# The last add level of the even transform residues in the product tables, and the skip weight in the first filter tap

## The reference

```
filt = hdn @ w4                                   # (length, 2 orders, 2 directions, 1024)
filt = filt * exp(-t * deltas)                    # t runs from 0 to 1, so the factor is 1 at tap 0
kcirc = concat([h_fwd, 0, h_bwd[:0:-1]])          # 2 * length taps
spec = rfft(z, 2 * length) * rfft(kcirc)
y = irfft(spec)[:length] + z * skip               # skip: one weight for each channel and order
zz = hx1 * long_conv(hv, filt[0], skip[0]);  zz = hx2 * long_conv(zz, filt[1], skip[1])
```

## Time and profile before

| | us |
|---|---|
| median of 3 runs | 3003.19 |
| the profiled execution | 3002.44 |
| its span | 3000.4 |
| PE busy | 2732.0 (91%) |
| DVE busy | 1526.7 (51%) |
| POOL busy | 411.0 (14%) |

### The profile page before, as it was taken

One profiled execution on the slowest core, in us unless ns is written; L12 is line 12 of the kernel. 1 busy time (PEld: TensorE's weight loads), 2 busy tenths in 40 slices (PEclk: granted clock), 3 DMA queues, 4 the chain that ended last, 5 costly groups with the idle time before them and its releaser, 6 DMA issues.

```text
span 3000.4 us, 33511 instructions
## 1 busy us (share of the span) xinstructions
PE 2732.0 (91%) x13372; PEld 1569.4 (52%) x13372; DVE 1526.7 (51%) x2153; ACT 813.9 (27%) x1672; POOL 411.0 (14%) x501
## 2 busy tenths in 40 slices
PE   5999999999999999788888888789399999999997
PEld 3444444766776666545555544445144444444487
DVE  6444331333323232389999999787482222222243
ACT  5333222343434334312222221112151111100132
POOL 0000000000000000133333334333010000000000
PEclk8999999999999999789999999899699999999999
DMA  5522221010101010300111111210631131000022
GB/s 208 204 81 94 82 81 50 26 50 26 51 27 49 26 50 16 117 25 32 32 60 60 32 35 42 84 50 28 207 109 49 43 116 39 15 28 29 29 91 85
DMA packets 103770, 191.91 MB, mean 64 GB/s; under 512 B 4919, under 2 KB 78895, under 8 KB 103360
## 3 DMA queue, kind: packets, MB, share of 16 engines
q1 hardware_dynamic: 88288, 114.93, 12.0%
q0 software_dynamic: 15184, 68.56, 6.1%
q10 hardware_dynamic: 144, 6.29, 0.6%
HBM read 141.43 MB, written 54.62 MB: 65 GB/s over the span
## 4 chain that ended last, share of the span: by engine, by line
PE 72%; DVE 18%; issue 6%; POOL 1%; ACT 1%; DMA 1%; SPq 0%; DVEq 0%; ACTq 0%; POOLq 0%
PE ps L1003 48%; PE ps L1272 8%; PE ps L1170 5%; DVE mem L1834 4%; PE ps L1132 3%; PE ps L1104 2%; PE ps L1117 2%; PE ps L1223 2%; DVE mem L1733 1%; DVE mem L1767 1%; DVE mem L1768 1%; DVE mem L1772 1%; PE ps L1165 1%; DVE mem L1933 0%; DVE mem L1777 0%
## 5 line engine op out<-in xcount | busy, mean ns | idle before, releaser
L1003 PE MATMUL ps<-mem 128*128 128x512 f16 (+1 forms) x8448 | 1545.3, 343 | 54.4 <-DVE mem L690 40.6
L1003 PEld LDWEIGHTS ps<-mem 128*128 128x128 f16 x8448 | 844.2, 103 | 716.9 <-issue 78.1
L1170 PE MATMUL ps<-mem 128*128 128x512 f32 (+1 forms) x1104 | 463.2, 577 | 60.0 <-DVE mem L1777 54.3
L1170 PEld LDWEIGHTS ps<-mem 128*128 128x128 f32 x1104 | 224.6, 208 | 293.9 <-issue 276.7
L1699 DVE TENSOR_TENSOR mem<-ps,mem 128x512 f32<-128x512 f32 (+2 forms) x144 | 79.8, 554 | 436.8 <-PE ps L1104 407.8
L1272 PE MATMUL ps<-mem 128*128 128x512 f32 x576 | 249.9, 592 | 0.9 <-DVE mem L1970 0.9
L1434 ACT ACTIVATE mem<-ps 128x512 f32<-128x512 f32 (+1 forms) x144 | 72.4, 503 | 411.2 <-PE ps L1117 411.2
L1272 PEld LDWEIGHTS ps<-mem 128*128 128x128 f32 x576 | 109.4, 190 | 133.4 <-issue 130.1
L664 ACT ACTIVATE mem<-mem 128x2048 f16<-128x2048 f32 x48 | 96.0, 2000 | 294.6 <-DVE mem L683 251.1
L690 DVE SCALAR_TENSOR_TENSOR mem<-mem 128x2048 f16<-128x2048 f32 x48 | 112.7, 2349 | 115.6 <-ACT mem L664 115.6
L1223 PE MATMUL ps<-mem 128*128 128x256 f32 x768 | 169.1, 379 | 0.0
(11 more groups left out here) (176 smaller groups left out, 2503.5 us busy)
## 6 DMA issues: line engine op xcount, KB each, us to landing
mem<-in_w_in SPq DMA_DIRECT2D x44, 1024.0 KB, 5.2
s_uc<-mem POOLq DMA_DIRECT2D x24, 768.5 KB, 3.8
mem<-s_uc SPq DMA_DIRECT2D x18, 1024.0 KB, 6.2
mem<-c_dec SPq DMA_DIRECT2D x12, 1024.0 KB, 5.0
s_og<-mem POOLq DMA_DIRECT2D x72, 132.0 KB, 2.0
mem<-s_og POOLq DMA_DIRECT2D x12, 792.0 KB, 5.0
s_hn<-mem POOLq DMA_DIRECT2D x1, 6912.0 KB, 19.6
mem<-s_hn SPq DMA_DIRECT2D x3, 2304.0 KB, 19.1
```

The source lines that it names most:

```text
L1003: mm = pe.matmul(out, lhs(a, k), rhs(b, k), start=(k == 0 and x == 0), stop=(k == KD - 1 and x == 2))
L1170: mm = pe.matmul(out, ftab[:, P * tab:P * tab + P], a[:, comp, :], start=(x == 0), stop=(x == len(terms) - 1))
```

## The change

Three things change. Lines are cut to the core.

The tables of planes A0 and A4: each table had one half of its columns zero; now the planes hold sums that are one add level less far along, and the tables of both planes are full (two more tables, 128 x 2176 words instead of 128 x 1920). The number and shape of the products stays.

```
-    c4, s4 = (A4, 0, add(cat(z, np.cos(ang(0, k4))))), (A4, 0, add(cat(z, -np.sin(ang(0, k4)))))
-    pairs.append(([(A0, 0, add(cat(co, z))), c4], [(A0, 0, add(cat(sz, z))), s4],
-                  [(A0, 0, add(cat(si, z))), s4], [(A0, 0, add(cat(cy, z))), c4]))
+    c4, s4 = np.cos(ang(0, k4)), -np.sin(ang(0, k4))
+    def even(m0, m4):
+        return [(A0, 0, add(cat(m0, m4))), (A4, 0, add(cat(m0, -m4)))]
+    pairs.append((even(co, c4), even(sz, s4), even(si, s4), even(cy, c4)))
...
-    r = np.concatenate([cat(np.cos(iang(k0)) * weight(k0), zi), cat(zi, np.cos(iang(k4)) * weight(k4))])
+    r = np.concatenate([cat(i0, i0), cat(i4, -i4)])
```

The butterflies (`butterfly`; `butterfly_shifted` in the same way) and the recombine lose that level:

```
-                chain(dve.tensor_tensor(e, f[:, 0:2 * w], f[:, 2 * w:4 * w], ALU.add))
-                chain(dve.tensor_tensor(a[:, A2R:A2N + 1, :], f[:, 0:2 * w].rearrange("p (a c) -> p a c", a=2),
-                                        f[:, 2 * w:4 * w].rearrange("p (a c) -> p a c", a=2), ALU.subtract))
-                settle()
-                e0, e1 = e[:, 0:w], e[:, w:2 * w]
-                chain(dve.tensor_tensor(A(A0), e0, e1, ALU.add))
-                chain(dve.tensor_tensor(A(A4), e0, e1, ALU.subtract))
+                chain(dve.tensor_tensor(a[:, A2R:A2N + 1, :], lower, upper, ALU.subtract))
+                chain(dve.tensor_tensor(a[:, A0:A4 + 1, :], lower, upper, ALU.add))
+                settle()
+                e1 = A(A4)
...
-                wait_free(dve, u0)
-                chain(dve.tensor_tensor(lane(E, 2, 0), lane(b0, 2, 0), lane(b0, 2, 1), ALU.add))
-                chain(dve.tensor_tensor(lane(E, 2, 1), lane(b0, 2, 0), lane(b0, 2, 1), ALU.subtract))
                 wait_free(dve, u1)
                 wait_free(dve, u3)
                 chain(dve.tensor_tensor(U, b3, b1, ALU.add))
                 chain(dve.tensor_tensor(V, b1, b3, ALU.subtract))
-                settle()
+                wait_free(dve, u0)
                 wait_free(dve, u2)
-                chain(dve.tensor_tensor(X, b2, E, ALU.add))
-                settle()
-                chain(dve.tensor_tensor(E, E, b2, ALU.subtract))
+                chain(dve.tensor_tensor(X, b2, b0, ALU.add))
+                chain(dve.tensor_tensor(E, b0, b2, ALU.subtract))
+                settle()
```

The skip weight goes into tap 0 of the forward filter. The decay there is 1, so row 0 of the decay tile holds the skip weights instead, and the tap is the filter product plus that row:

```
-                sp.dma_start(dec_of(i), cst[f"dec{s}"][:, per * FQ * q:per * FQ * (q + 1)].rearrange("(t p) c -> p t c", p=P)
-                             ).then_inc(ld_dec, 16)
+                d, c = dec_of(i), slice(per * FQ * q, per * FQ * (q + 1))
+                sp.dma_start(d[0:1, 0, :], ins["hyena_skip"][0, o:o + 1, c]).then_inc(ld_dec, 16)
+                sp.dma_start(d[1:P, 0, :], cst[f"dec{s}"][1:P, c]).then_inc(ld_dec, 16)
+                sp.dma_start(d[:, 1:, :], cst[f"dec{s}"][P:LENS[s], c].rearrange("(t p) c -> p t c", p=P)).then_inc(ld_dec, 16)
...
-                    dve.wait_ge(ld_dec, 16 * (i + 1))
+                    dve.wait_ge(ld_dec, 48 * (i + 1))
...
-                    op = dve.memset(h[0:1, FQ:2 * FQ], 0.0)
+                    chain(dve.memset(h[0:1, FQ:2 * FQ], 0.0))
+                    op = dve.tensor_tensor(h[0:1, 0:FQ], ps[0:1, n % 2, 0:FQ], d[0:1, 0, :], ALU.add)
...
-                for x in range(rows_):
-                    sk = CS + KD * o + chans(i)[0] + rows_ * h + x
-                    chain(dve.scalar_tensor_tensor(y[:, x, :], z[:, x, :], cols[:, sk:sk + 1], y[:, x, :], ALU.mult, ALU.add))
-                settle()
```

More of the change, by code:

```diff
@@ L157, in dft @@
     k0, k4 = 8 * np.arange(h), 4 + 8 * np.arange(h)
-    z, zi = np.zeros((P, h)), np.zeros((h, w))
     co, si = np.cos(ang(0, k0)), -np.sin(ang(0, k0))
@@ L161, in dft @@
     sz[:, 0] = cy[:, 0] = nyq
-    c4, s4 = (A4, 0, add(cat(z, np.cos(ang(0, k4))))), (A4, 0, add(cat(z, -np.sin(ang(0, k4)))))
-    pairs.append(([(A0, 0, add(cat(co, z))), c4], [(A0, 0, add(cat(sz, z))), s4],
-                  [(A0, 0, add(cat(si, z))), s4], [(A0, 0, add(cat(cy, z))), c4]))
+    c4, s4 = np.cos(ang(0, k4)), -np.sin(ang(0, k4))
+    def even(m0, m4):
+        return [(A0, 0, add(cat(m0, m4))), (A4, 0, add(cat(m0, -m4)))]
+    pairs.append((even(co, c4), even(sz, s4), even(si, s4), even(cy, c4)))
     s0 = -np.sin(iang(k0)) * weight(k0)
     s0[0] = nyq / n
-    r = np.concatenate([cat(np.cos(iang(k0)) * weight(k0), zi), cat(zi, np.cos(iang(k4)) * weight(k4))])
-    s = np.concatenate([cat(s0, zi), cat(zi, -np.sin(iang(k4)) * weight(k4))])
+    i0, i4 = np.cos(iang(k0)) * weight(k0), np.cos(iang(k4)) * weight(k4)
+    t4 = -np.sin(iang(k4)) * weight(k4)
+    r = np.concatenate([cat(i0, i0), cat(i4, -i4)])
+    s = np.concatenate([cat(s0, s0), cat(t4, -t4)])
     units[0] += [(0, 0, addi(r), 0, 2 * w), (0, 1, addi(s), 0, 2 * w)]
@@ L273, in build @@
         BASE = top[0]
-        CW, CB, CG, CS = 0, 9 * KD, 12 * KD, 13 * KD
-        NCOLS = 15 * KD
+        CW, CB, CG = 0, 9 * KD, 12 * KD
+        NCOLS = 13 * KD
         ssq, rstd = small[:, 0:NT], small[:, NT:2 * NT]
@@ L343, in build @@
         hx = grid(2, SP)
-        e01 = grid(2, 2 * FQ)
+        odd = part(2 * FQ)
         iv_u, iv_v, iv_a, iv_b = (hs[:, n, :] for n in range(4))
@@ L730, in _ @@
                              (ins["conv_b"][0].rearrange("(c p) -> c p", p=P), 3 * KD),
-                             (ins["pre_norm_g"][0].rearrange("(c p) -> c p", p=P), KD),
-                             (ins["hyena_skip"][0].rearrange("o (c p) -> (o c) p", p=P), 2 * KD)):
+                             (ins["pre_norm_g"][0].rearrange("(c p) -> c p", p=P), KD)):
                 sp.dma_start(rows[r0:r0 + cnt, :], src).then_inc(S["ld_small"], 16)
@@ L833, in _ @@
                 sp.dma_start(xres[t % 2], src).then_inc(ld_xr[t % 2], 16)
-        NSMALL, NTABS = 16 * 13, 16 * 7
+        NSMALL, NTABS = 16 * 12, 16 * 7
         @block.gpsimd
@@ L1761, in butterfly @@
                 f = src.rearrange("p t c -> p (t c)")
-                e = e01.rearrange("p a c -> p (a c)")
                 def A(c):
                     return a[:, c, :]
-                chain(dve.tensor_tensor(e, f[:, 0:2 * w], f[:, 2 * w:4 * w], ALU.add))
-                chain(dve.tensor_tensor(a[:, A2R:A2N + 1, :], f[:, 0:2 * w].rearrange("p (a c) -> p a c", a=2),
-                                        f[:, 2 * w:4 * w].rearrange("p (a c) -> p a c", a=2), ALU.subtract))
+                lower, upper = (f[:, 2 * w * n:2 * w * n + 2 * w].rearrange("p (a c) -> p a c", a=2) for n in range(2))
+                chain(dve.tensor_tensor(a[:, A2R:A2N + 1, :], lower, upper, ALU.subtract))
+                chain(dve.tensor_tensor(a[:, A0:A4 + 1, :], lower, upper, ALU.add))
                 settle()
-                e0, e1 = e[:, 0:w], e[:, w:2 * w]
-                chain(dve.tensor_tensor(A(A0), e0, e1, ALU.add))
-                chain(dve.tensor_tensor(A(A4), e0, e1, ALU.subtract))
+                e1 = A(A4)
                 chain(dve.scalar_tensor_tensor(A(A1R), A(A2N), RT, f[:, 0:w], ALU.mult, ALU.add))
@@ L1794, in butterfly_shifted @@
                 settle()
-                chain(dve.tensor_tensor(e01, a[:, A1R:A1N + 1, :], a[:, A3R:A3I + 1, :], ALU.add))
+                chain(dve.tensor_tensor(a[:, A0:A4 + 1, :], a[:, A1R:A1N + 1, :], a[:, A3R:A3I + 1, :], ALU.add))
                 chain(dve.tensor_tensor(a[:, A2R:A2N + 1, :], a[:, A1R:A1N + 1, :], a[:, A3R:A3I + 1, :], ALU.subtract))
@@ L1799, in butterfly_shifted @@
                 settle()
-                chain(dve.tensor_tensor(a[:, A0, :], e01[:, 0, :], e01[:, 1, :], ALU.add))
-                chain(dve.tensor_tensor(a[:, A4, :], e01[:, 0, :], e01[:, 1, :], ALU.subtract))
                 chain(dve.scalar_tensor_tensor(a[:, A1R, :], f[0], RT, f[4], ALU.mult, ALU.add))
@@ L1900, in recombine @@
                 U, V, E, X = iv_u, iv_v, iv_a, iv_b
-                G = e01[:, 0, :]
+                G = odd
                 settle()
@@ L1912, in recombine @@
                 chain(dve.tensor_tensor(V, b1, b3, ALU.subtract))
+                wait_free(dve, u0)
+                wait_free(dve, u2)
+                chain(dve.tensor_tensor(X, b2, b0, ALU.add))
+                chain(dve.tensor_tensor(E, b0, b2, ALU.subtract))
                 settle()
-                wait_free(dve, u2)
-                chain(dve.tensor_tensor(X, b2, E, ALU.add))
-                settle()
-                chain(dve.tensor_tensor(E, E, b2, ALU.subtract))
                 chain(dve.tensor_tensor(lane(G, 2, 0), lane(V, 2, 0), lane(U, 2, 1), ALU.subtract))
```

## The result

The changed kernel takes 2974.2 us (median of 4 runs, 2972.14 to 2976.19) against 3003.24 before: a ratio of 0.9901, 95% interval 0.9889 to 0.9914. The forecast was 2974.0. The profiled execution took 2972.14 us with a span of 2970.3. Another set of 5 runs gave 2974.19.

The account below looks back on a forecast made before the run. DVE was taken to bound the long items' first half and the wide items, PE hardly behind DVE in the second half; -0.3 + 3.9 - 14.2 - 4.4 + 11.1 - 25.6 = -29.5, giving 2974 us (64%), range 2953 to 2988.

Parts of the forecast that it names:

- Kernel's start: Start of the kernel: one issue ahead of the input loads goes, -0.3 us.
- DVE's work: Butterflies, recombine heads and skips save 95 us, one-row adds cost 5: net 90 us of DVE's own time.
- Item 0's decay load: Hyena stage's start: 127 rows on one DMA engine cost +5.9 us; with two shorter first butterflies, +3.9.
- Seven long boundaries: Items 1 to 7: first butterfly saves 8.5 us, slack 5.7, together -14.2; other DVE savings become waiting for PE.
- the slack: Long items' second half: DVE's lateness beyond 3.08 us after PE's pair start, summing to 5.7 us over seven boundaries.
- Item 7 to 8: Boundary where PE has no next pair loaded: shorter butterfly, skip, wait and recombine work give -4.4 us in all.
- Item 9's decay load: Waited-for load before item 9: 127 rows on one engine cost +11.3 us, less 0.2 for ready spectra: +11.1.
- Wide items: Items 9 to 11, DVE's time counts in full: -8.4, -8.0 and, in the last item, -9.2; together -25.6 us.
- spread rows: Rival: the 127 rows are spread, so both waited decay loads cost 0.9 us each; 2958 us, 20%.
- all of DVE's saving counts: Rival: DVE's whole 90 us saving reaches the time, with the slow loads; 2930 us, 5%.
- PE's second half: Rival: in long items PE's second half runs at full clock after shorter idling, 2.7 us off each of seven; 2955, 7%.
- far slower single-engine rows: Rival: single-engine rows go far below 20 GB/s in the two waited decay loads, slower than before; 3032 us at 0.2 us per KB, 4%.

Follow-up runs that it names:

- 112 + 15: Changed kernel with the decay load's 127-row piece loaded as 112 and 15 rows, one DMA more per item; 2957.61 us.
- 96 + 31: Changed kernel with the decay load's 127-row piece loaded as 96 and 31 rows; 2959.64 us.
- the six adds: Changed kernel plus six unused 512-wide DVE adds behind the second recombine of items 0 to 6, about 30 us of work; 2974.21 us.
- before with three loads: Kernel before with only the decay load cut into pieces of 1, 127 and the rest of the rows; 3019.51 us, ratio 1.0052.
- tables alone: Changed kernel's butterflies, recombines and tables, with the skip, its small load and the decay load as in the kernel before; 2967.97 us.
- the kernel with its own row: Changed kernel with the skip row in its own buffer and the decay tile in one load again; 2957.3 us, ratio to before 0.9847.
- an earlier load: Own-buffer skip row kernel with item 9's decay load issued ahead of the filter weights' loads; 2957.67 us against 2957.3.

## Why the prediction was right, step by step

- *Kernel's start, -0.3.* The input loads' issues moved from 5.08 to 4.70 us, -0.4. The further lead at the stage's start is scatter, as said, and it flatters the profiled execution by some 2 us.
- *DVE's work, -90.* Measured -88.7. The recombine's head, priced at 2.54 us, takes 1580.99 - 1578.45 = 2.54. The one-row add takes 0.35 us, 0.28 from start to start (priced at 0.33), and lies in PE's pair.
- *Item 0's decay load, +5.9, with what comes off +3.9.* A grew by 6.05, and with the two first butterflies off, the first product came 4.0 us later relative to the stage's start, forecast +3.9.
- *Seven long boundaries, -14.2.* P fell by 12.8 in one profiled execution and 13.6 in the other. Of the 1.4 us missing in the first, 0.7 lie in DVE's half (from the product to PE's release it lost 7.8 us where 8.5 were priced), 0.4 in the slack (the product now starts 3.13 us after the pair, not 3.08) and 0.3 in PE's run. The period is 71.6 us, forecast 71.5. That the rest of DVE's saving turns into a wait of 5 to 6 us is shown twice over: by the wait of 5.47, and by thirty microseconds of work that fit into it without changing the time.
- *Item 7 to 8, -4.4.* From item 7's first product to SP's issue of load 9 it took 1875.69 - 1807.10 = 68.6 us instead of 1890.60 - 1818.02 = 72.6: -4.0.
- *Item 9's decay load, +11.1.* From SP's first issue of it (the skip row's now, at 1879.35) to the filter tile it took 19.1 us instead of 6.8, +12.3. Forecast 11.3, of which 0.4 for issues and the rest by a rate of 22.5 GB/s. Reckoned the same way, the 12.3 for 240 KB more are 20.7 GB/s and the 6.05 for 120 KB 21.7, the lower part of the 20 to 25 that were estimated. The Trainium skill ("DMA: Bandwidth & Descriptors", "Why a DMA increments its semaphore by 16 and not by 1") names 127 partitions as a case of one engine; by its rule of the largest divisor up to 16, 112 rows go to 16 engines, 15 rows to 15 and 31 rows to one. The DMA share of 0.06 behind the 127 rows, the 16.6 us won by 112 + 15 and B's 3.1 us with 96 + 31 agree.
- *Wide items, -25.6.* W fell by 17.9, and from the filter tile that uses load 9 to item 8's last gate it takes 1948.19 - 1898.47 = 49.7 instead of 1959.18 - 1901.06 = 58.1 us, -8.4: -26.3. By stretches, up to item 8's last gate and from there gate to gate, it is -8.4, -7.5, -7.9 and -2.4. The prediction has three numbers for these four stretches, -8.4, -8.0 and -9.2. They fit if its "last item" stands for the last two stretches, which lost 10.3; taken for item 11 alone, one stretch was left out and the last priced at nearly four times what it gave, and the near hit of this term is luck. One such item takes 50.4 to 51.2 us, forecast 50.5, and PE sets this time, where the prediction had DVE and POOL.

Of the rivals, spread rows would have given 2958, and the two kernels in which they are spread take 2957.3 and 2957.6: its price was right and its condition was not. That all of DVE's saving counts is refuted by the six adds. PE's second half did not reach full clock: the 36 records took 9.7 to 10.5 us after the shorter idle time, against 9.6 to 10.6 before, and the sum of the seven runs from butterfly to pair is 227.4 us against 227.1. This rival took the idle time of 7.02 to shrink by 1.2; it shrank by 1.7 on average and by 2.5 to 2.9 where it was 7.02, since part of the slack comes off it as well, and even that did not suffice. The rival of far slower single-engine rows is out by the measured 20.7 GB/s.

What went wrong is small: three terms missed by 0.7 to 1.4 us in both directions. As measured, the terms add up to -27.2 us in the first profiled execution and -28.0 in the second, and the medians differ by 29.0. The rest lies outside the terms, 1.2 us of it behind the stage, where no instruction changed. There the three kernels that keep the skip operation and its load (before, before with three loads, tables alone) take 884.2 to 884.6 us from item 11's last gate to the end, and the ten others 881.9 to 883.4; no run shows why. The total was met closer than the terms deserve, and that is luck.

## What to carry to other kernels

When two engines take turns as the bound within a period, price an edit by the half it lies in: here one add counted in full ahead of PE's release and not at all behind it. A tile without its first row is 127 rows, and here loads of 127 and of 31 rows behaved as loads on one engine, up to 12.3 us late; give the odd row a place of its own, or split the rest so that it divides, which was worth 16.6 to 16.9 us here. Look also at which loads are waited for: ten of the twelve cost nothing. And ask of a wait whether another engine started as late: of the 12.6 us that DVE waited for the decay tile, the 2.7 that an earlier load took away were worth nothing, since PE had waited as long for its weights and bounded what followed.

## What the runs showed of the hardware

**SP's issues take longer behind a load on one engine.** The issue of the decay load takes 0.37 to 0.39 us in the kernel with its own row. Behind the 127-row piece the issue of the rest takes 0.89 to 4.46 us in the twelve items, 4.46 before item 9, and there the four issues of filter weights behind it take 6.97 us instead of 3.50. The loads that SP issues next start later by as much: the issue of the rest ended at 1884.62 us, and ahead of it the DMA share was 0.06. What this costs by itself no run separates from the load on one engine.

**DVE and POOL hold each other up.** The two POOL operations that close an item's products run beside the first butterfly, in the half that counts. Timelines of DVE and POOL of the changed kernel:

```profile
1548.90 1.22 DVE L1773 TENSOR_TENSOR mem<-mem 128x1024 f32<-128x1024 f32 x1
1550.04 2.29 DVE L1774 TENSOR_TENSOR mem<-mem 128x1024 f32<-128x1024 f32 x1
1552.36 1.64 DVE L1777 SCALAR_TENSOR_TENSOR mem<-mem 128x512 f32<-128x512 f32 x1
1553.92 0.68 DVE L1778 SCALAR_TENSOR_TENSOR mem<-mem 128x512 f32<-128x512 f32 x1
...
1543.32 1.28 POOL L936 TENSOR_TENSOR mem<-mem 128x512 f32<-128x512 f32 x1
...
1549.13 2.12 POOL L935 TENSOR_TENSOR mem<-mem 128x512 f32<-128x512 f32 x1 [1.30 <-DVE mem L1845]
1551.21 2.24 POOL L936 TENSOR_TENSOR mem<-mem 128x512 f32<-128x512 f32 x1
```

L1774 takes 2.29 us here and 1.22 in the third butterfly, where POOL is idle; L1777 1.64 and 0.69; POOL's two take 2.12 and 2.24 instead of 1.28. That is 2.0 us of DVE per long item in the half that counts, and it was there before the change (2.29 and 1.64 us at 1553.93 and 1556.26 us of its trace). The Trainium skill ("SBUF — State Buffer", "SBUF: two separate sides") says that a DVE operation with two SBUF inputs and a POOL operation that reads SBUF lock each other out for a whole operation. That fits: POOL's first operation lasts until 1551.25 us, L1774 ends 1.1 us after that, POOL's second again 1.1 us later, and L1777 0.55 us after it, so each waits for the other's end and then takes about its time alone. A kernel that moves those two POOL operations or the butterfly apart was not tried; it stays open what of the 2 us it would give.
